# Rotary part of the MLA queries: the rotation summed in the score product, or before it

## The reference

```
def apply_rope(x, cos, sin):
    x1, x2 = jnp.split(xf, 2, axis=-1)
    out = jnp.concatenate([x1 * cos - x2 * sin, x2 * cos + x1 * sin], axis=-1)
...
    q = (rms_norm(c_q, q_norm) @ w_uq).reshape(B, S, MLA_HEADS, MLA_NOPE_DIM + MLA_ROPE_DIM)
    q_nope, q_pe = q[..., :MLA_NOPE_DIM], q[..., MLA_NOPE_DIM:]
    q_pe = apply_rope(q_pe, cos[:, None, :], sin[:, None, :])
    k_pe = apply_rope(k_pe, cos, sin)
...
        logits = (jnp.einsum('bqhd,bkhd->bhqk', q_nope[:, q0:q1], k_nope[:, :q1])
                  + jnp.einsum('bqhr,bkr->bhqk', q_pe[:, q0:q1], k_pe[:, :q1]))
```

## Time and profile before

| | us |
|---|---|
| median of 3 runs | 1159.79 (1159.53 to 1159.91) |
| the profiled execution | 1159.91 |
| its span | 1158.1 |
| TensorE busy | 1133.7 (98%) |
| VectorE busy | 573.9 (50%) |
| ScalarE busy | 397.4 (34%) |
| GpSimd busy | 171.9 (15%) |

### The profile page before, as it was taken

One profiled execution on the slowest core, in us unless ns is written; L12 is line 12 of the kernel. 1 busy time (PEld: TensorE's weight loads), 2 busy tenths in 40 slices (PEclk: granted clock), 3 DMA queues, 4 the chain that ended last, 5 costly groups with the idle time before them and its releaser, 6 DMA issues.

```text
span 1158.1 us, 14678 instructions
## 1 busy us (share of the span) xinstructions
PE 1133.7 (98%) x5110; PEld 911.2 (79%) x5110; DVE 573.9 (50%) x863; ACT 397.4 (34%) x685; POOL 171.9 (15%) x126
## 2 busy tenths in 40 slices
PE   6999999999999999999999999999999999999995
PEld 4888888888887888777777788888888888888873
DVE  6644344443445436786555554445443354334444
ACT  5322222322235225684344433333321232222242
POOL 4111001100114202330000002321110011101133
PEclk9999999999999999999999999999999999999997
DMA  6234323332324222112221223322233223322221
GB/s 217 91 96 107 115 91 102 97 91 91 107 71 126 91 98 73 56 37 74 73 67 62 73 91 98 103 91 91 91 94 105 93 91 94 105 91 91 81 64 73
DMA packets 32301, 105.68 MB, mean 91 GB/s; under 512 B 3889, under 2 KB 5329, under 8 KB 32257
## 3 DMA queue, kind: packets, MB, share of 16 engines
q1 hardware_dynamic: 31824, 104.29, 28.1%
q0 software_dynamic: 192, 0.78, 0.6%
q10 hardware_dynamic: 240, 0.05, 0.0%
HBM read 102.22 MB, written 2.88 MB: 91 GB/s over the span
## 4 chain that ended last, share of the span: by engine, by line
PE 95%; DVE 2%; ACT 1%; DMA 0%; issue 0%; POOL 0%; DVEq 0%; SPq 0%; POOLq 0%; ACTq 0%
PE bank L1084 30%; PE bank L1086 29%; PE bank L1085 29%; PE bank L1202 1%; PE bank L1234 1%; PE bank L1259 1%; PE bank L1193 1%; DVE xg_lo L733 1%; PE bank L1244 1%; PE bank L1145 0%; DMA staged<-in_ffn_w 0%; DVE x L1077 0%; DVE w_lo L726 0%; PE bank L1137 0%; POOL h_lo L390 0%
## 5 line engine op out<-in xcount | busy, mean ns | idle before, releaser
L1084 PE MATMUL bank<-xg_hi,w_hi 128*128 128x512 f32 x1024 | 407.0, 398 | 10.1 <-DVE xg_lo L733 8.9
L498 ACT ACTIVATE w_hi<-staged 128x1024 fp32r<-128x1024 f32 x192 | 203.5, 1060 | 589.4 <-PE bank L1086 589.4
L1086 PE MATMUL bank<-xg_hi,w_lo 128*128 128x512 f32 x1024 | 399.9, 391 | 0.0
L1085 PE MATMUL bank<-xg_lo,w_hi 128*128 128x512 f32 x1024 | 399.8, 390 | 0.0
L726 DVE TENSOR_TENSOR w_lo<-staged,w_hi 128x1024 fp32r<-128x1024 f32 x192 | 236.5, 1232 | 101.6 <-ACT w_hi L498 101.3
L1084 PEld LDWEIGHTS bank<-xg_hi,w_hi 128*128 128x128 f32 x1024 | 192.7, 188 | 59.0 <-issue 13.6
L1086 PEld LDWEIGHTS bank<-xg_hi,w_lo 128*128 128x128 f32 x1024 | 192.8, 188 | 41.1
L1085 PEld LDWEIGHTS bank<-xg_lo,w_hi 128*128 128x128 f32 x1024 | 193.0, 188 | 38.8 <-issue 0.7
L390 POOL TENSOR_TENSOR h_lo<-hid,h_hi 128x512 f32 x44 | 71.2, 1617 | 571.4 <-ACT h_hi L521 542.6
L1084 PE MATMUL bank<-h_hi,w_hi 128*128 128x512 f32 x352 | 139.5, 396 | 0.1
L1085 PE MATMUL bank<-h_lo,w_hi 128*128 128x512 f32 x352 | 139.3, 396 | 0.0
(11 more groups left out here) (129 smaller groups left out, 869.7 us busy)
## 6 DMA issues: line engine op xcount, KB each, us to landing
staged<-in_ffn_w SPq DMA_DIRECT2D x119, 512.0 KB, 3.3
staged<-in_w_gate SPq DMA_DIRECT2D x16, 512.0 KB, 3.2
staged<-in_w_in SPq DMA_DIRECT2D x15, 512.0 KB, 3.3
staged<-in_ffn_w SPq DMA_DIRECT2D x16, 384.0 KB, 3.1
staged<-in_w_ob SPq DMA_DIRECT2D x8, 512.0 KB, 3.2
staged<-in_w_out SPq DMA_DIRECT2D x8, 512.0 KB, 3.3
x<-in_x_t SPq DMA_DIRECT2D x8, 256.0 KB, 6.2
staged<-in_w_oa SPq DMA_DIRECT2D x4, 512.0 KB, 3.3
```

The lines of the kernel that those rows point to most:

```text
L498: nc.scalar.activation(w_hi[:, u % SPLIT, :], staged[:, u % STAGED, :], ACT.Copy).then_inc(hi_done, 1)
L1084: nc.tensor.matmul(o, wh, hi, start=start, stop=False)
L1085: nc.tensor.matmul(o, wh, lo, start=False, stop=False)
L1086: return nc.tensor.matmul(o, wl, hi, start=False, stop=stop)
```

## The change

The rotary part of a query is now rotated before the score product, and summed. For each uq tile ScalarE copies the 64 plain rows from PSUM into `qm`, VectorE multiplies the 32 rotary rows by the cosines into `qm` and the 32 swapped rows by the sines into `rot`, and GpSimd adds `rot` to `qm`. Two semaphores are new: `q_nope` (ScalarE's copy; VectorE's second product waits for it) and `q_ready` (GpSimd's sum; VectorE's next second product waits for it, and the scores of that head). The score product contracts 96 rows. The key is laid into rows 64 to 95 only, so one copy (L963) goes, and the kpe product makes 64 rows from half the weights. The two rotary products of the key no longer wait for each other.

```diff
@@ -215,6 +215,7 @@
         vband_banked, vband_ready = sem("vband_banked"), sem("vband_ready")
+        q_nope, q_ready = sem("q_nope"), sem("q_ready")
         s_ready, s_step, max_ready, exp_done = sem("s_ready"), sem("s_step"), sem("max_ready"), sem("exp_done")
@@ -451,6 +452,11 @@
                         .then_inc(kpe_ready, 1)
+                elif kind == "uq":
+                    alone(q_ready, t + 1)
+                    pool.wait_ge(grp_read, MIX_G + G_UQ + t + 1)
+                    pool.tensor_tensor(qm[rope_rows, t, :], qm[rope_rows, t, :], rot[rope_rows, :], ALU.add)\
+                        .then_inc(q_ready, 1)
 
@@ -653,6 +659,10 @@
                     nc.scalar.activation(vm[:, t, :], filler_bank(G_UV + t)[:, :], ACT.Copy).then_inc(grp_read, 1)
+                elif kind == "uq":
+                    act.wait_ge(grp_ready, g + G_UQ + t + 1)
+                    nc.scalar.activation(qm[0:NOPE, t, :], filler_bank(G_UQ + t)[0:NOPE, :], ACT.Copy)\
+                        .then_inc(q_nope, 1)
                 elif kind == "gate" and part == 1:
@@ -948,29 +958,32 @@
 
-                    cos_rows, sin_rows = slice(NOPE, NOPE + ROPE), slice(NOPE + ROPE, P)
-                    nc.vector.tensor_tensor(rot[NOPE:P, :], filler_bank(G_KPE)[NOPE:P, :], rms[NOPE:P, :],
+                    nc.vector.tensor_tensor(rot[0:2 * ROPE, :], filler_bank(G_KPE)[0:2 * ROPE, :], rms[0:2 * ROPE, :],
                                             ALU.mult).then_inc(grp_read, 1)
                     dve.wait_ge(grp_read, gg + 1)
-                    nc.vector.tensor_tensor(km[cos_rows, 0, :], rot[cos_rows, :], rope_sb[cos_rows, :], ALU.mult)\
+                    nc.vector.tensor_tensor(km[NOPE:NOPE + ROPE, 0, :], rot[0:ROPE, :], rope_sb[0:ROPE, :], ALU.mult)\
                         .then_inc(kpe_step, 1)
-                    dve.wait_ge(kpe_step, 1)
-                    nc.vector.tensor_tensor(rot[cos_rows, :], rot[sin_rows, :], rope_sb[sin_rows, :], ALU.mult)\
-                        .then_inc(kpe_step, 1)
+                    nc.vector.tensor_tensor(rot[NOPE:NOPE + ROPE, :], rot[ROPE:2 * ROPE, :], rope_sb[ROPE:2 * ROPE, :],
+                                            ALU.mult).then_inc(kpe_step, 1)
                 elif kind == "uk":
+                    dve.wait_ge(kpe_ready, 1)
+                    for h in range(max(2 * t, 1), 2 * t + 2):
+                        nc.vector.tensor_copy(km[NOPE:NOPE + ROPE, h, :], km[NOPE:NOPE + ROPE, 0, :])\
+                            .then_inc(kpe_ready, 1)
+                elif kind == "uq":
+                    gg = g + G_UQ + t
+                    b = filler_bank(G_UQ + t)
+                    lo, hi = slice(NOPE, NOPE + ROPE), slice(NOPE + ROPE, P)
+                    dve.wait_ge(grp_ready, gg + 1)
                     if t == 0:
+                        dve.wait_ge(grp_read, gg)
+                    nc.vector.tensor_tensor(qm[lo, t, :], b[lo, :], rope_sb[lo, :], ALU.mult)
+                    if t >= 1:
+                        dve.wait_ge(q_ready, t)
+                    else:
                         dve.wait_ge(kpe_ready, 1)
-                        nc.vector.tensor_copy(km[NOPE + ROPE:P, 0, :], km[NOPE:NOPE + ROPE, 0, :])\
-                            .then_inc(kpe_ready, 1)
-                        dve.wait_ge(kpe_ready, 2)
-                    for h in range(max(2 * t, 1), 2 * t + 2):
-                        nc.vector.tensor_copy(km[NOPE:P, h, :], km[NOPE:P, 0, :]).then_inc(kpe_ready, 1)
-                elif kind == "uq":
-                    dve.wait_ge(grp_ready, g + G_UQ + t + 1)
-                    if t == 0:
-                        dve.wait_ge(grp_read, g + G_UQ)
-                    nc.vector.tensor_tensor(qm[:, t, :], filler_bank(G_UQ + t)[:, :], rope_sb[:, :], ALU.mult)\
-                        .then_inc(grp_read, 1)
+                    dve.wait_ge(q_nope, t + 1)
+                    nc.vector.tensor_tensor(rot[lo, :], b[hi, :], rope_sb[hi, :], ALU.mult).then_inc(grp_read, 1)
                 elif kind == "gate" and part == 1:
@@ -1197,9 +1210,10 @@
                     if i == 0:
-                        pe.wait_ge(grp_read, g + G_UQ + h + 1)
-                        pe.wait_ge(kpe_ready, MH + 1)
-                    nc.tensor.matmul(b[:, 0:query_keys(i)], qm[:, h, norm_rows(i)], km[:, h, 0:query_keys(i)],
+                        pe.wait_ge(q_ready, h + 1)
+                        pe.wait_ge(kpe_ready, MH)
+                    rows = slice(0, NOPE + ROPE)
+                    nc.tensor.matmul(b[:, 0:query_keys(i)], qm[rows, h, norm_rows(i)], km[rows, h, 0:query_keys(i)],
                                      start=True, stop=True).then_inc(s_ready, 1)
@@ -1271,13 +1285,14 @@
 
-            def half_product(uu, r, half):
+            def half_product(uu, r, half, width=P):
 
                 if half == 0:
                     unit_ready(uu)
                     next_bank(r)
                 for k in range(4 * half, 4 * half + 4):
-                    last = three(filler_bank(r)[:, :], slice(k * P, (k + 1) * P), uu, *from_x(k), k == 0, k == KD - 1)
+                    last = three(filler_bank(r)[0:width, :], slice(k * width, (k + 1) * width), uu, *from_x(k),
+                                 k == 0, k == KD - 1)
                 if half == 1:
@@ -1285,7 +1300,7 @@
                 elif kind == "kpe":
-                    half_product(u + U_KPE, G_KPE, part)
+                    half_product(u + U_KPE, G_KPE, part, 2 * ROPE)
                 elif kind == "gate":
@@ -1395,7 +1410,7 @@
     cos, sin = np.cos(ang), np.sin(ang)
-    rope = np.concatenate([np.ones((NOPE, S)), cos, cos, -sin, sin]).astype(np.float32)
+    rope = np.concatenate([cos, cos, -sin, sin] * 2).astype(np.float32)
     mask = np.zeros((P, P), np.float32)
@@ -1420,7 +1435,7 @@
     kpe = w_in[:, kv0:q0]
-    kpe = np.concatenate([kpe, kpe[:, swap]] * 2, axis=1)
+    kpe = np.concatenate([kpe, kpe[:, swap]], axis=1)
     uq = w_uq.reshape(QR, MH, NOPE + ROPE)
@@ -1439,7 +1454,7 @@
             out[f"ffn{n}_{w}"] = tiles(a[f"ffn{n}_{w}"][0])
-    out.update(w_in=tiles(big), w_kpe=kpe.reshape(KD, P, P).transpose(1, 0, 2).reshape(P, -1),
+    out.update(w_in=tiles(big), w_kpe=kpe.reshape(KD, P, 2 * ROPE).transpose(1, 0, 2).reshape(P, -1),
                w_uk=uk.transpose(1, 0, 2).reshape(P, -1), w_uv=uv.reshape(P, -1), w_uq=uq.reshape(3, P, UNIT),
```

## The result

The changed kernel takes 1167.41 us (median of 4 runs, 1166.52 to 1167.56), the kernel before 1159.85 in the same runs (1159.53 to 1159.92): a ratio of 1.0062, 95% interval 1.0049 to 1.0075. It is 7.6 us slower. The forecast was 3.5 us slower, and the time lies 1.1 us above the range.

A forecast was written before the change was run, and what follows sets the result against it. TensorE work was taken to bound the kernel (95% of the chain). Terms 1.14 + 2.20 + 0.5 - 0.3 = +3.5 us on the profiled 1159.91 gave 1163.4, or 1163.3 by the median; range 1161.3 to 1166.3.

The forecast's parts named there:

- The joints: Transposes of steps 14 and 15 wait for GpSimd's normalisation, delayed by its additions: +1.14 and +2.20 us.
- the key part: Rotary key on VectorE: a copy and a wait between products go, shortening TensorE's wait for lat: -0.3 us, bounds 0 and -0.4.
- The rings: Uq tiles 2 to 7: each tile's circle of VectorE, GpSimd and ScalarE work gives short TensorE waits at steps 19 and 20: +0.5 us.
- the race against normalise L910: VectorE's normalise starts 0.10 us after the product, GpSimd's addition 0.14; if GpSimd wins, the bound is +3 us.
- rival D: Steps 17 to 20 each wait because GpSimd's additions come before normalise: +3 on the forecast, 1166.3; chance 0.16.
- the ring of about 4.1 us: One tile's circle, second product to next second product, with GpSimd's addition holding nmax: about 4.1 us against TensorE's 3.5 us step.
- No term for the clock: The added delay was to stay unchanged behind the waits, as TensorE has no idle time there; no clock change was priced.
- TensorE's wait for lat: The 0.4 us TensorE wait for the lat product, at the end of the rotary key's chain, was to become 0.1.
- The 0.1 us for the wait that goes between the two products: VectorE's rotary key products, no longer waiting for each other, were to follow after 0.62 us, not 0.69 and a signal.
- The narrower products: Key matmuls loading 64 columns and scores over 96 rows on TensorE: taken as 0, with -1.3 or +3.2 us if loads mattered.
- rival C: Score and key matmul time goes by the active part of the array: -3.7 us in sum, 1156.2; chance 0.02.

The follow-up runs named there:

- Experiment 4: Changed kernel with useless TensorE matmuls in passes 14 and 15 and GpSimd's additions of tiles 2, 4 to 7 waiting for VectorE's normalisation: 1162.52 us.
- Experiment 1: Changed kernel with GpSimd's additions of uq tiles 2, 4, 5, 6 and 7 waiting until VectorE's normalisation has ended: 1163.89 us.
- experiment 9: Changed kernel with VectorE's second product over all 128 rows, sine part of the queries left out: 1165.44 us.
- experiments 3: Changed kernel with 11 useless TensorE matmuls (3, 5 and 3) where it waits in steps 14 and 15: 1166.35 us.
- experiment 5: Changed kernel with only the key's part and narrower products kept; query tiles made by one 128-row VectorE product, no sum: 1159.26 us.
- experiment 6: Changed kernel with the second product written to its own rows 96 to 127, sine part of the queries left out: 1166.35 us.
- experiment 10: Kernel before with its one product per query tile cut in two (rows 0 to 95 and 96 to 127): 1161.3 us.

## Why the prediction was wrong

The side was right: slower, by GpSimd's place ahead of two normalisations. The forecast was less than half of the measured 7.6 us, and two terms are to blame.

**The joints: right.** Predicted +1.14 and +2.20, measured +1.22 and +2.17. The wait has another form: TensorE stops twice in each step, at the scores, for the sum, and at the transposes, for the normalisation. The sum took 1.25 to 1.29 us, smax was held (0.67), the copy was what tile 1's second product waited for (0.36). Experiment 4, where only this and the key part are left, is 2.9 us slower: 3.39 - 0.40 = 3.0.

**The rings: the step that failed.** "Tiles 2 to 7 ... **+0.5 us**", bounds 0 and +3, "if GpSimd wins the race against normalise L910". It came to +3.4, a little over the upper bound. I had VectorE win a race by 0.04 us, put rival D at 0.16, and took the value next to the good end. The hold was put on the wrong operation: the ring of about 4.1 us has the sum hold nmax, but an MLA nmax (128x1) was not held (0.15 us at 524.00, inside the sum), and what is held is the normalisation L920 ahead of it. Without that hold there is no wait in the rings (experiments 1 and 4), so a won race costs nothing, and the +0.5 had no cause either. Experiment 1 shows the term: 3.5 us go with five waits on GpSimd and nothing else. Rival D is what happened, and it was priced as the rare case only for want of a row where a VectorE operation of that length had a lead of 0.04 us. The one row there was, sinkd, is 0.16 us long.

There were two errors in the race. The normalisation starts 0.24 us after the second product ends and not 0.10: the new product is followed after 0.73 us and not 0.60 as the 128-row one at 538.75 was. And a lead of 0.04 would not have helped: in experiment 9 it was there and L920 was held. The prediction's "In the trace a small VectorE operation that starts within a GpSimd operation ends with it" was true of the row it had, and too wide for nmax of 128x1 and too narrow for L920.
The Trainium skill (SBUF — State Buffer, 🔬 SBUF: two separate sides) says that between GpSimd and a VectorE operation in a two-port mode or with two SBUF inputs, whichever starts first gets the port pair for the whole instruction and the other blocks. The exclusive hold agrees with this case's rows, in both directions (L920 1.32 us for 0.35; GpSimd 1.87 for 1.04 at 465.04), and products that read PSUM are not held; "starts first" can't be read off recorded starts as close as these, since L920 at 536.39 was held by the sum at 536.43.

**No term for the clock.** The prediction had none, and said that the delay stays as it is. In the profile 1.61 us come after the waits of step 15, at a granted clock of 0.54. Over 11 runs of the kernel after, four at a mean clock of 0.994 took 1165.27 to 1166.68 and seven at 0.991 to 0.993 took 1167.29 to 1167.64; experiments 3 and 4 gain 1.1 and 1.4 us by useless matmuls in the waits. So this term is 1.1 to 1.6 us where it comes (the rings take back 0.4 of it), and the median holds it.

**The key part: -0.40 for -0.3.** TensorE's wait for lat shrank by 0.3, as forecast, and 0.1 came from the narrower products. The 0.1 us for the wait that goes between the two products did not exist. After, they follow each other in 0.71 us without a wait:

```profile
489.21 0.68 DVE L964 TENSOR_TENSOR km<-rot,rope_sb 32x512 f32<-32x512 f32 x1
489.92 0.68 DVE L966 TENSOR_TENSOR rot<-rot,rope_sb 32x512 f32<-32x512 f32 x1
490.63 0.16 DVE L913 TENSOR_TENSOR den<-den,sinkd 128x4 f32<-128x4 f32 x1
```

Before it was 0.72 with the wait (490.39 to 491.11); the 0.62 was a row of another pair. **The narrower products: nearly right.** Key matmuls keep their 0.23 us, scores their distances (experiment 5), and rival C had nothing. But the first matmul of each half is followed after 0.29 us (480.69 to 480.98) where before it was 0.34 (486.60 to 486.94): 0.1 us in the two halves together, where the prediction took 0.

With the ring term at 3.4 and the clock term of this profile, 1.6, the forecast's own sum is 3.34 + 3.4 + 1.6 - 0.3 = 8.0, against 7.6 between the medians and 8.0 between the profiles without their start-up (6.95 + 1.07). The 0.4 is not resolved: 21 runs of the kernel before spread from 1158.07 to 1160.27.

Two things stay open. What decides between VectorE and GpSimd at small leads wasn't separated further: sinkd with a lead of 0.03 us ran free, L920 with 0.03 or 0.04 was held five times (experiment 9), w_lo with 0.26 ran free. And why the clock falls behind the same idle times in one execution and not in another isn't known.

## What to carry to other kernels

An operation given to the idle GpSimd is not free for VectorE: each one can hold a VectorE operation on SBUF for its whole length (here sums, scalings and remainders of 4 to 1024 columns, not those that read PSUM), so price it as on VectorE's queue wherever the two are released by the same event, and place it behind the operation that TensorE needs. Where the sum hangs on a race of under 0.1 us, forecast the lost race and take the other as the rival. And new waits of TensorE of about 1 us are worth a clock term of their own: here 1.1 to 1.6 us, in some executions.

## What the hardware showed that was not expected

- A VectorE product of 512 columns is recorded with 0.69 us and followed by a next instruction that does not wait for its result after 0.60 to 0.62 us if both begin at row 0 (535.59 to 536.20 in experiment 9), and after 0.70 to 0.73 if the next one begins at another row than it does: 516.46 to 517.18 after, whatever rows it writes (experiment 6); a pair of 96 and 32 rows takes 1.43 (experiment 10). The number of rows does not explain it: the 128-row product L771 on SBUF is followed by a copy from row 64 after 0.72 us (498.46 to 499.18 after), and three copies of 32 rows, all from row 64, take 1.09 us where one takes 0.42. That the first row is the cause was not tried by a run of its own.
- GpSimd's sum of 32x512 takes 1.25 to 1.29 us. It and GpSimd's normalisation hold VectorE operations of 4 columns as well as of 1024: smax L891 0.16 to 0.67, L920 (128 columns) 0.29 to 1.27, w_lo 1.22 to 1.77. Not seen held were the reciprocal L914 (0.18), nmax of 128x1 (0.15), and what reads PSUM (L980, L986, L897).
- A held operation ends after GpSimd's by 0.14 to 0.21 us less than it takes when free: 0.02 us for one that takes 0.16, 0.08 for 0.29, 0.15 for 0.35, 0.22 for 0.42, 1.08 for the w_lo of 1.22 (539.70 to 541.32 in experiment 1, the sum ends at 540.24). It does so wherever within GpSimd's it starts, and L920 also when it starts 0.04 us ahead.
- A TensorE that idled 1.10 and 0.61 us in one step got 3.4 us at the 1.2 GHz level in the profiles of after and of experiment 1, and not in that of experiment 6.
